# Gated unit of a decoder step: the gate half's chunks first, the norm and the spatial products between the other half's chunks, the spatial bias added on VectorE

## The reference, cut to what matters

```python
def _chunk_spatial(v, w_s, b_s):
    n, t, c = v.shape
    nch = -(-t // CHUNK)
    tp = nch * CHUNK
    vp = jnp.pad(v, ((0, 0), (0, tp - t), (0, 0))).reshape(n, nch, CHUNK, SG_GROUPS, SG_GROUP_DIM)
    w = w_s * jnp.tril(jnp.ones((CHUNK, CHUNK), w_s.dtype))
    y = jnp.einsum('gij,nkjgc->nkigc', w, vp) + b_s.T[None, None, :, :, None]
    return y.reshape(n, tp, c)[:, :t]

def _chunk_mixer(x, w_in, ln_g, ln_b, w_s, b_s, w_o):
    u, v = jnp.split(jax.nn.gelu(x @ w_in), 2, axis=-1)
    v = _layer_norm(v, ln_g, ln_b)
    return (u * _chunk_spatial(v, w_s, b_s)) @ w_o, v
```

## Time and profile before

| | us |
|---|---|
| median of 3 runs | 3419.72 (3414.72 to 3422.53) |
| the profiled execution, its own time | 3419.5 |
| its span, first to last instruction | 3417.7 |
| TensorE busy, by the page | 3289.0 (96%) |
| VectorE busy | 2468.0 (72%) |
| ScalarE busy | 1462.5 (43%) |
| GpSimd busy | 894.0 (26%) |

### The profile page before, as it was taken

One profiled execution on the slowest core, in us unless ns is written; L12 is line 12 of the kernel. 1 busy time (PEld: TensorE's weight loads), 2 busy tenths in 40 slices (PEclk: granted clock), 3 DMA queues, 4 the chain that ended last, 5 costly groups with the idle time before them and its releaser, 6 DMA issues.

```text
span 3417.7 us, 54652 instructions
## 1 busy us (share of the span) xinstructions
PE 3289.0 (96%) x19630; PEld 3114.2 (91%) x19630; DVE 2468.0 (72%) x5134; ACT 1462.5 (43%) x2581; POOL 894.0 (26%) x690
## 2 busy tenths in 40 slices
PE   8988989999999999999998898999999999999998
PEld 7933489999999999999997788999999999999997
DVE  3243258878888878888884327888888878888887
ACT  3222233356666633333333314336666663333333
POOL 3211110010121344545441001002012234445552
PEclk9988999999999999999998879999999999999999
DMA  4254523466787999999981112247678799999994
GB/s 141 91 164 120 158 71 104 139 213 233 273 285 263 338 377 396 377 374 377 376 299 61 56 38 81 97 160 246 238 253 297 286 347 394 391 372 380 369 385 157
DMA packets 315827, 835.35 MB, mean 244 GB/s; under 512 B 32248, under 2 KB 155256, under 8 KB 311440
## 3 DMA queue, kind: packets, MB, share of 16 engines
q1 hardware_dynamic: 233472, 541.63, 45.0%
q0 software_dynamic: 82192, 291.85, 23.5%
HBM read 726.25 MB, written 107.11 MB: 244 GB/s over the span
## 4 chain that ended last, share of the span: by engine, by line
PE 91%; DVE 3%; ACT 2%; DMA 2%; issue 1%; SPq 0%; POOLq 0%; ACTq 0%; POOL 0%; DVEq 0%
PE pstr L1656 30%; PE aux L1733 16%; PE pstr L1733 16%; PE pstr L1445 15%; PE aux L1691 5%; PE pstr L1567 2%; PE pstr L1587 2%; PE aux L1476 1%; PE aux L1485 1%; DMA wraw<-in_v 1%; PE aux L1646 1%; PE pstr L1540 1%; PE aux L1787 1%; PE aux L1786 1%; DVE rstd L1000 0%
## 5 line engine op out<-in xcount | busy, mean ns | idle before, releaser
L967 DVE TENSOR_TENSOR wlo<-wraw,whi 128x1024 fp32r<-128x1024 f32 x600 | 734.0, 1224 | 596.0 <-ACT whi L699 593.5
L699 ACT ACTIVATE whi<-wraw 128x1024 fp32r<-128x1024 f32 x600 | 632.3, 1055 | 308.1 <-PE pstr L1733 198.9
L1656 PE MATMUL pstr<-xh,whi 128*128 128x392 f32 x2048 | 717.8, 350 | 0.0
L1656 PE MATMUL pstr<-xl,whi 128*128 128x392 f32 x2048 | 696.7, 340 | 0.0
L1656 PE MATMUL pstr<-xh,wlo 128*128 128x392 f32 x2048 | 695.8, 340 | 0.0
L672 POOL DMA_INDIRECT rows<-in_ur,idx x256 | 332.7, 1299 | 1378.5 <-DVE hs L1202 822.8
L672 POOL DMA_INDIRECT rows<-in_v,idx x256 | 427.9, 1672 | 425.0 <-DVE ysum L1215 324.2
L1656 PEld LDWEIGHTS pstr<-xh,whi 128*128 128x128 f32 x2048 | 385.1, 188 | 0.1
L1656 PEld LDWEIGHTS pstr<-xl,whi 128*128 128x128 f32 x2048 | 385.1, 188 | 0.0
L1656 PEld LDWEIGHTS pstr<-xh,wlo 128*128 128x128 f32 x2048 | 384.5, 188 | 0.0
L1733 PE MATMUL aux<-wth,whi 128*128 128x392 f32 x1024 | 349.9, 342 | 8.6 <-DVE wtl L1251 8.5
(11 more groups left out here) (240 smaller groups left out, 5287.0 us busy)
## 6 DMA issues: line engine op xcount, KB each, us to landing
wraw<-in_u SPq DMA_DIRECT2D x256, 512.0 KB, 4.4
wraw<-in_v SPq DMA_DIRECT2D x256, 512.0 KB, 7.6
hidden<-hid SPq DMA_DIRECT2D x256, 196.0 KB, 2.8
gates<-gst SPq DMA_DIRECT2D x28, 1792.0 KB, 8.2
hl<-hidden SPq DMA_DIRECT2D x256, 196.0 KB, 8.2
gc<-gates SPq DMA_DIRECT2D x64, 784.0 KB, 12.2
wraw<-in_w SPq DMA_DIRECT2D x88, 512.0 KB, 3.5
kv<-in_ck SPq DMA_DIRECT2D x32, 256.0 KB, 3.1
```

The costliest lines, as they stand in the source:

```text
L699: e.activation(whi[:, s % RING, :], wraw[:, s % RING, :], ACT.Copy).then_inc(w_hi, 1)
L967: e.tensor_tensor(wlo[:, s % RING, :], wraw[:, s % RING, :], whi[:, s % RING, :].bitcast(F32), ALU.subtract).then_inc(w_lo, 1)
L1656: mm = e.matmul(pstr[:, r % 2, 0, 0:ND], w[:, r, k * P:(k + 1) * P], x[:, k, 0:ND], start=k == 0 and w is whi and x is xh, stop=k == KB - ...
```

## The change

The weight chunks of the gated unit are laid out with v's half first, so chunks 0 to 7 are v and 8 to 15 are u. The mean blocks of v follow chunks 2 to 9. The rest is put between u's chunks, on each engine in the same order: after chunk 9 the centring and the first two squares, after chunk 10 the variance, root, reciprocal and multiplication, after chunks 11 and 12 the scaling (four blocks each), after chunk 12 the first two turns, after chunks 13 and 14 two spatial products with two turns each, after chunk 15 the last four products and two turns. The bias matmuls are gone: VectorE adds the bias to the product in SBUF (into the block of v that is no longer needed), waits for its own instruction, and multiplies u by it. The mask of `ws` moves to chunk 7, and the multiplication of the 8 sample columns into `mix`.

```diff
+MEANS_AT, SQUARES_AT, TURNS_AT = 2, KB + 2, KB + 4
+def spatial_by(n):
+    return min(KB, max(0, 2 * (n - TURNS_AT)))
...
 # ScalarE (norm split into squares, deviation, rescale)
+            for n in range(N_INC):
+                e.wait_ge(chunk_done, C_INC + n + 1)
+                out = uv[:, (n + KB) % N_INC, :].rearrange("p (h n) -> p h n", h=2)
+                e.activation(out, pstr[:, n % 2, :, 0:HALF], ACT.Gelu_apprx_tanh).then_inc(chunk_taken, 1)
+                round_next(C_INC + n)
+                if n == SQUARES_AT - 1:
+                    squares(2, v_half, range(0, 2))
+                if n == SQUARES_AT:
+                    squares(2, v_half, range(2, KB))
+                    deviation(2)
+                if n == SQUARES_AT + 1:
+                    rescale(2, v_half, V_SG, V_SG + 8, v_half, range(0, KB // 2))
+                if n == SQUARES_AT + 2:
+                    rescale(2, v_half, V_SG, V_SG + 8, v_half, range(KB // 2, KB))
+                if n == TURNS_AT:
+                    take_turned(0)
+                    take_turned(1)
+                for g in range(spatial_by(n - 1), spatial_by(n) if n + 1 < N_INC else KB - 2):
+                    if g + 2 < KB:
+                        take_turned(g + 2)
+            for g in range(KB):
+                e.wait_ge(mix_ready, 2 * (g + 1))
+                round_x(uv, [g])
...
 # VectorE (norm split into centre, normalise)
+            def mix(g):
+                e.wait_ge(sg_done, g + 1)
                 e.tensor_tensor(uv[:, g, SEQ:N], uv[:, g, SEQ:N], sps[:, g, :], ALU.mult).then_inc(mix_ready, 1)
+                biased = uv[:, KB + g, 0:SEQ]
+                own.mark(e.tensor_tensor(biased.rearrange("p (t n) -> p t n", t=QT), aux[:, 2 + g % 2, :].rearrange("p (t n) -> p t n", t=QT),
+                                         spread(bs[:, g, :], 1, (P, QT, P)), ALU.add))
+                own.settle()
+                e.tensor_tensor(uv[:, g, 0:SEQ], uv[:, g, 0:SEQ], biased, ALU.mult).then_inc(mix_ready, 1)
+            for n in range(N_INC):
+                split_next(C_INC + n)
+                if n == KB - 1:
+                    e.wait_ge(sgu_in, 32)
+                    e.tensor_tensor(ws[:], ws[:], spread(c(UTRI), 1, (P, KB, P)), ALU.mult).then_inc(ws_masked, 1)
+                if n == SQUARES_AT - 1:
+                    centre(2, v_half, aux[:, 0:2])
+                if n == SQUARES_AT:
+                    normalise(2, v_half)
...
+                for g in range(spatial_by(n - 1), spatial_by(n) if n + 1 < N_INC else KB):
+                    mix(g)
+                    if g >= KB - 4:
+                        split_x(4, uv, [g - (KB - 4)])
+            split_x(4, uv, range(4, KB))
...
 # TensorE
-            stage(C_INC, N_INC, 3, (uv[:, KB:2 * KB, :], 2))
-            variance(2)
...
+            def spatial(g):
                 e.wait_ge(st_ready, g + 1)
                 if g >= 2:
-                    e.wait_ge(mix_ready, KB + g - 1)
+                    e.wait_ge(mix_ready, 2 * (g - 1))
                 for t in range(QT):
                     dst = aux[:, 2 + g % 2, t * P:(t + 1) * P]
-                    e.matmul(dst, vnt[:, g % 2, t * P:(t + 1) * P], ws[:, g, :], start=True, stop=False)
-                    mm = e.matmul(dst, c(ONES, P, 1), bs[0:1, g, :], start=False, stop=True)
+                    mm = e.matmul(dst, vnt[:, g % 2, t * P:(t + 1) * P], ws[:, g, :], start=True, stop=True)
                 mm.then_inc(sg_done, 1)
+            for n in range(N_INC):
+                chunk(C_INC + n, taken(C_INC) + n, n % RING, 3 if n == 0 else None)
+                if MEANS_AT <= n < MEANS_AT + KB:
+                    mm = mean_block(uv[:, KB:2 * KB, :], n - MEANS_AT, aux[:, 0:2])
+                    if n == MEANS_AT + KB - 1:
+                        mm.then_inc(ln_mean, 1)
+                if n == SQUARES_AT:
+                    variance(2)
+                if n == TURNS_AT:
+                    turn(0)
+                    turn(1)
+                    e.wait_ge(ws_masked, 1)
+                for g in range(spatial_by(n - 1), spatial_by(n) if n + 1 < N_INC else KB):
+                    spatial(g)
+                    if g + 2 < KB:
+                        turn(g + 2)
             stage(C_WOC, N_WO, 4, (res, 3))
```

More of the change, by code:

```diff
@@ L719, in round_x, with squares @@
                     e.activation(xh[:, k, :], src[:, k, :], ACT.Copy).then_inc(x_hi, 1)
-            def norm(n, src, gcol, bcol, dst):
-                for k in range(KB):
+            def squares(n, src, blocks):
+                for k in blocks:
                     e.wait_ge(ln_centred, 8 * n + k + 1)
@@ L727, in norm, with deviation, rescale @@
                     e.activation(sq[:, k % 2, :], src[:, k, :], ACT.Square).then_inc(ln_sq, 1)
+            def deviation(n):
                 e.wait_ge(ln_var, 8 * n + 8)
                 e.activation(halves(rstd[:]), aux[:, 2:4, 0:HALF], ACT.Sqrt, bias=vec[:, V_EPS:V_EPS + 1]).then_inc(ln_root, 1)
-                for k in range(KB):
+            def rescale(n, src, gcol, bcol, dst, blocks):
+                for k in blocks:
                     e.wait_ge(ln_normed, 8 * n + k + 1)
@@ L735, in norm @@
                     e.activation(dst[:, k, :], src[:, k, :], ACT.Identity, bias=bias, scale=scale).then_inc(ln_out, 1)
+            def norm(n, src, gcol, bcol, dst):
+                squares(n, src, range(KB))
+                deviation(n)
+                rescale(n, src, gcol, bcol, dst, range(KB))
             e.wait_ge(setup_in, 64)
@@ L942, in _, with take_turned @@
             norm(1, res, V_LN + 16, V_LN + 24, xt)
[L943 to L950, removed]
-                if g >= 2:
-                    e.wait_ge(mix_ready, KB + g - 1)
-                    round_x(uv, [g - 2])
+            def take_turned(g):
+                e.wait_ge(st_done, g + 1)
+                if g >= 2:
+                    e.wait_ge(sg_done, g - 1)
+                e.activation(vnt[:, g % 2, :], aux[:, g % 2, :], ACT.Copy).then_inc(st_ready, 1)
+            v_half = uv[:, KB:2 * KB, :]
+            for n in range(N_INC):
[21 more added lines that the diff above has]
+                round_x(uv, [g])
             round_stage(C_WOC, N_WO)
@@ L991, in add_stage, with centre @@
                     split_next(s)
-            def norm(n, src, mean, split=None):
+            def centre(n, src, mean):
                 e.wait_ge(ln_mean, n + 1)
@@ L998, in norm, with normalise @@
                     e.tensor_tensor(s, s, mean[:, :, 0:HALF], ALU.subtract).then_inc(ln_centred, 1)
+            def normalise(n, src, split=None):
                 e.wait_ge(ln_root, n + 1)
@@ L1007, in norm @@
                     split_x(split, xt, [KB - 2, KB - 1])
+            def norm(n, src, mean, split=None):
+                centre(n, src, mean)
+                normalise(n, src, split)
             e.wait_ge(setup_in, 64)
@@ L1407, in _ @@
             norm(1, res, aux[:, 0:2], 3)
[L1408 to L1416, removed]
@@ L1417, in _ @@
-            own.settle()
-            for g in range(KB):
-                e.tensor_tensor(uv[:, g, SEQ:N], uv[:, g, SEQ:N], sps[:, g, :], ALU.mult).then_inc(mix_ready, 1)
[L1420 to L1425, removed]
+            def mix(g):
+                e.wait_ge(sg_done, g + 1)
+                e.tensor_tensor(uv[:, g, SEQ:N], uv[:, g, SEQ:N], sps[:, g, :], ALU.mult).then_inc(mix_ready, 1)
+                biased = uv[:, KB + g, 0:SEQ]
[3 more added lines that the diff above has]
+                e.tensor_tensor(uv[:, g, 0:SEQ], uv[:, g, 0:SEQ], biased, ALU.mult).then_inc(mix_ready, 1)
@@ new lines, in _ @@
+            v_half = uv[:, KB:2 * KB, :]
+            for n in range(N_INC):
[8 more added lines that the diff above has]
+                if n == TURNS_AT:
+                    for g in range(KB):
+                        e.wait_ge(ln_out, 8 * 2 + g + 1)
+                        own.mark(e.tensor_scalar(sps[:, g, :], uv[:, KB + g, SEQ:N], vec[:, V_W00 + g:V_W00 + g + 1],
+                                                 vec[:, V_B00 + g:V_B00 + g + 1], ALU.mult, ALU.add))
+                    own.settle()
+                for g in range(spatial_by(n - 1), spatial_by(n) if n + 1 < N_INC else KB):
+                    mix(g)
+                    if g >= KB - 4:
+                        split_x(4, uv, [g - (KB - 4)])
@@ L1764, in _ @@
             variance(1)
-            stage(C_INC, N_INC, 3, (uv[:, KB:2 * KB, :], 2))
-            variance(2)
-            e.wait_ge(ws_masked, 1)
             def turn(g):
@@ L1849, in lay_out @@
         "w": f(np.concatenate([chunks(w_in_ab[0][:, :cols]), chunks(w_o_ab[0]), chunks(peer_wq[0]),
-                               chunks(w_in_c[0]), chunks(w_o_c[0]), chunks(peer_wq[1])])),
+                               chunks(w_in_c[0])[KB:], chunks(w_in_c[0])[:KB], chunks(w_o_c[0]), chunks(peer_wq[1])])),
         "u": f(peer_u.reshape(DEPTH * P, P, KB, P).transpose(0, 3, 2, 1)),
```

## The result

| | before | changed |
|---|---|---|
| median of four runs, us | 3418.97 (3414.72 to 3422.53) | 3369.07 (3366.68 to 3376.41) |
| profiled execution, its own time | 3419.5 | 3376.41 |
| chunk 10 taken to first output chunk added | 118.2 | 57.9 |
| mean clock over the span | 0.973 | 0.979 |

The ratio is 0.9858 with a 95% interval of 0.9839 to 0.9877: the changed kernel is faster by 49.9 us. Five more runs on another occasion gave 3367.93.

The account below looks back on a forecast made before the run. TensorE was taken as the bound; rebuilding the span from input chunk 10 to the first output chunk saves 53.2 us and table loading adds 0.1: 3419.5 - 53.2 + 0.1 = 3366.4 us, range 3359 to 3378.

Parts of the forecast that it names:

- The bound: Whole kernel: TensorE carries 91% of the chain, and its own list sets the pace in the gated unit.
- Prices on TensorE: Rebuilt span: chunk 5.77 us, mean block 0.88, variance 8.1, turn 0.44, group of four spatial products 0.88.
- rounds: Behind chunks 13 and 14: two products and two turns on TensorE, 2.6 us each time.
- The dearer end: Spatial products: 1.44 us a group instead of 0.88, plus 3.4 us, 3370; chance 0.12 together with a dearer mix.
- Do the other engines keep up?: Between u's chunks: ScalarE and VectorE deliver in time, slack 1.6 us at the tightest point, so TensorE does not wait.
- The mix: VectorE's sample-column multiplication, bias addition and multiplication by u: 1.45 us together, low end 1.3, high end 2.2.
- The tail: Chunk 15's end to first output chunk's end, 1943.5 to 1958.3: VectorE's mixes and rests decide, 3.7 us beyond TensorE alone.
- this rival: TensorE's clock falls to half in the tail: plus 2.9 us and up to 2.4 more, 3369 to 3372; chance 0.2.
- Gelu's and the root's table: ScalarE's extra table switch: a 1.28 us load in the layer's norm replaces a 1.23 wait, plus 0.1 us.
- The rivals: Cases beside the forecast (0.6): clock falling in the tail or between chunks, dearer products or mix, products at old pace.
- The clock between the chunks: Small float32 work drops the clock among chunks: 3397 if input stage only (chance 0.03), 3434 if both stages (0.02).

Follow-up runs that it names:

- The late scaling: Changed kernel with all eight scalings behind chunk 12 instead of four behind chunk 11 and four behind chunk 12; one run, 3368.54 us.
- removing VectorE from the way: Changed kernel with three products behind chunks 13 and 14, two behind 15, mixes first, and own memory for the output stage's input; 3361.19 us, ratio 0.9831.

## Why the prediction was right

**The bound.** Right. The chain stayed TensorE's up to chunk 15 and went through VectorE in the tail, as forecast, and 53.3 us less on it in the rebuilt part was forecast as 53.2. The median is 2.7 us above the forecast of 3366.4, the second one 1.5; the execution that was profiled was 10.1 us slower outside the part. Runs of the changed kernel lie up to 11 us apart, so the distance is the better test of the sum than the close total.

**Prices on TensorE.** Right: variance 8.03 (8.1), turn 0.44, product 0.89 (0.88), rounds of 2.65 (2.6). The dearer end, 1.44 a group, was 0.72 halved; at full clock a product beside a bias matmul takes 0.41, which is more than half of 0.72, and without its neighbour 0.22.

**Do the other engines keep up?** Right. No instruction of TensorE waits between chunks 11 and 15. The late scaling shows what the cover is worth: a wait of 2.35 us cost 4.0.

**The mix.** 1.40 from one mix to the next in the rounds, 1.45 forecast; the addition 0.68 (0.69), the wait for itself 0.03 (0.04).

**The tail.** 14.9 against 14.8. That VectorE holds it was forecast as 3.7 us; removing the additions gave 2.5 back, removing VectorE from the way 4.3 in all. That the clock falls there happened, in one profiled execution of the changed kernel and not in the other, at the same distance of 57.9. In the other one it is 1.00 in each stretch from 1948 to 1964 (columns as in the earlier trace rows), and by its timeline TensorE waits for the fourth rest, the step on which the sum was built:

```profile
1956.00:1960.00 4.00, 2.97 (x23) 2.59 (x22) 3.96 (x9) 1.27 (x2) 0.00 (x0) 1.00 0.02 4
```

```profile
1958.70 0.51 PE L1502 MATMUL pstr<-xh,whi 128*128 128x260 f32 x2 [1.03 <-DVE xl L1020]
```

Where the clock fell, TensorE did not wait there: it spent that time on the chunk's first two steps at half clock, and the clock was back before the fourth step at 1961.95 (TensorE's timeline):

```profile
1960.83 0.58 PE L1502 MATMUL pstr<-xh,wlo 128*128 128x260 f32 x2
1961.24 0.40 PE L1502 MATMUL pstr<-xh,whi 128*128 128x260 f32 x2
...
1961.95 0.40 PE L1502 MATMUL pstr<-xh,whi 128*128 128x260 f32 x2
```

My price for this rival, 2.9 to 5.3, had the last five steps at half clock. They ran at full clock, and in this execution the rival cost nothing that the distance shows.

**Gelu's and the root's table.** The layer's norm shows the load and the root (ScalarE's timeline after):

```profile
2021.11 1.28 ACT L739 ACT_TABLE_LOAD   x1
2022.40 0.69 ACT L739 ACTIVATE rstd<-aux,vec 128x520 f32<-128x520 f32 x1
```

The last square to the root was 1.23 of waiting and is 1.31: plus 0.1, as forecast. The Trainium skill, "ScalarE: Activation LUTs", What ACT_TABLE_LOAD costs, gives some 1.38 us of drain for each switch. Here the load starts 0.02 behind the last square and the root 0.01 behind the load, so no such drain shows.

**The rivals.** The clock between the chunks did not fall, but the reason that spoke for it was misread. I took the 0.50 from 1952 to 2006 as what small float32 work gets; it was what the alternation of full products with one-row bias matmuls gets, and the change removes that. Where only the order is changed, the rival comes true by half: the clock falls with the products, but the chunks, at 7.45 and 6.97 in place of 5.77, bring it back each time. The Trainium skill, "TensorE: Matmul & The Clock Gate", A second HAM failure mode: psum-queue depth-cycling, describes such a swing for short idle times between groups; the order-alone run shows the swing, 0.50, 0.91, 0.50, with TensorE shown busy for 4.00 of 4.

**Where the gain comes from.** Taking away the bias matmuls alone saves 37.2 us of time, the order alone 15.7, both together 49.9. By distance, net of the moved means, they are 38.6, 22.4 (118.2 - 88.8 - 7.0, from that fast execution) and 53.3. The larger part was the bias, which the forecast's sum did not separate. With the bias on full rows, the order saves 84.0 - 61.5 - 7.0 = 15.5 of distance; without bias matmuls it saves 53.3 - 38.6 = 14.7, or 49.9 - 37.2 = 12.7 of time. By time the order's worth is of one size with and without the one-row matmuls, 15.7 and 12.7.

## What to carry to other kernels

Look at the granted clock of every stretch before believing a busy engine: 52 us at "busy" and 0.50 were in large part the price of one operand's shape, and one changed line, the same bias from full rows, gave 29 us back. When an order is changed and an operation removed at once, run each alone; here each had its share, 37 and 16 us, and the forecast alone, though it came true, did not tell them apart. What VectorE must do between the last input chunk and the first output chunk is worth its own memory, so that it can be done earlier; that gave 4.3 us of distance here, while the lower median is not clear of the runs' scatter.

## What the runs showed of the hardware that was not expected

A float32 matmul of one row that alternates with full ones of 128 columns made both take 0.41 to 0.42 at full clock, where full rows in the same alternation took 0.22, and the granted clock fell to 0.50 under it while TensorE was shown busy all the time. The same single row once a group, 512 columns wide, took 1.05 and left the clock at 1.00. What in this pairing brings the clock down, the runs do not separate.
